# Two layers written out, sums of squares beside the adds, half of the next layer's adaLN weights read beside the router, and half-row scatter-adds

## What is computed

```python
mod = silu(cond) @ w_ada[l] + b_ada[l]              # adaLN: 6 x 1024 numbers per token group
shift1, scale1, gate1, shift2, scale2, gate2 = split(mod, 6)
h = rmsnorm(x, norm1_g) * (1 + scale1) + shift1
proj = h @ w_in[l]                                  # q, k, v, conv, pool, u, v, gates
branches = attention(...), conformer_conv(...), multiscale_pool(...), spatial_gating(...)
x = x + gate1 * (sum(sigmoid(z_gate) * (branch @ w_branch)) @ w_out[l])
h2 = rmsnorm(x, norm2_g) * (1 + scale2) + shift2
aff = softmax(h2 @ w_router[l])                     # 16 experts
gate, idx = top_k(aff.T, 2 * L // 16)               # each expert picks 64 latent and 16 context tokens
y[e] = (silu(h2[idx[e]] @ w1[e]) * (h2[idx[e]] @ w3[e])) @ w2[e] * gate[e]
x = x + gate2 * scatter_add(y, idx)
# after two layers: out = rmsnorm(x, final_g)
```

## Time and profile before

| | us |
|---|---|
| median of 3 runs | 3164.21 |
| lowest, highest | 3155.08, 3170.53 |
| the profiled execution's own time | 3167.31 |
| its span, first to last instruction | 3165.6 |

### The profile page before, as it was taken

How to read it: one execution, slowest core, us unless ns; L and a number is a source line. 1 busy time by engine, 2 the same in 40 slices (tenths; PEclk the granted TensorE clock), 3 DMA queues, 4 the chain that set the end, 5 groups by cost and what they waited for, 6 DMA issues and landing times.

```text
span 3165.6 us, 70846 instructions
## 1 busy us (share of the span) xinstructions
PE 2835.2 (90%) x32596; PEld 2067.1 (65%) x32596; DVE 893.1 (28%) x1513; ACT 495.5 (16%) x862; POOL 270.9 (9%) x290
## 2 busy tenths in 40 slices
PE   6999999999995898998679999999999868898994
PEld 3554576765753788888535456766666458888883
DVE  3953222332114011111159432223221231111113
ACT  3012122332002000000020120233310120000001
POOL 1240000000000001010003200000000000001010
PEclk9999999999997999999889999999999989999997
DMA  7222301012122999999752223011120249999994
GB/s 315 106 113 107 121 30 59 30 56 100 41 80 95 365 401 402 402 401 402 309 222 93 96 107 120 30 59 40 72 87 27 106 168 356 399 405 401 408 403 165
DMA packets 56295, 609.08 MB, mean 192 GB/s; under 512 B 6832, under 2 KB 6832, under 8 KB 22000
## 3 DMA queue, kind: packets, MB, share of 16 engines
q1 hardware_dynamic: 38736, 550.52, 43.2%
q0 software_dynamic: 8448, 24.78, 3.1%
q10 hardware_dynamic: 8992, 32.11, 2.7%
HBM read 577.49 MB, written 29.88 MB: 192 GB/s over the span
## 4 chain that ended last, share of the span: by engine, by line
PE 65%; DMA 23%; DVE 9%; issue 2%; ACT 1%; SPq 0%; POOL 0%; POOLq 0%; DVEq 0%; ACTq 0%
PE ps L292 54%; DMA ring<-in_w_exp 19%; DVE region_b L1047 4%; PE ps L535 2%; DMA ring<-in_w_mix 2%; PE ps L508 1%; PE ps L518 1%; PE ps L589 1%; PE ps L572 1%; PE ps L662 1%; DMA region_x<-ffn_rows 1%; DVE rstd L1004 1%; DMA region_b<-h_rows,rstd 0%; DVE rstd L996 0%; DMA ffn_rows<-region_b,rstd 0%
## 5 line engine op out<-in xcount | busy, mean ns | idle before, releaser
L292 PE MATMUL ps<-hT,ring 128*128 128x320 f32 (+2 forms) x3600 | 1022.3, 442 | 21.5 <-DVE region_b L1035 11.5
L292 PE MATMUL ps<-region_r,ring 128*64 128x80 f32 x24192 | 898.8, 234 | 108.1 <-DMA ring<-in_w_exp 88.7
L292 PEld LDWEIGHTS ps<-region_r,ring 128*64 128x64 f32 x24192 | 867.0, 138 | 141.5 <-DMA ring<-in_w_exp 110.3
L292 PEld LDWEIGHTS ps<-hT,ring 128*128 128x128 f32 x3600 | 612.2, 192 | 382.7 <-issue 239.7
L292 PE MATMUL ps<-region_b,ring 128*128 128x320 f32 (+2 forms) x896 | 257.5, 439 | 3.5 <-DMA ring<-in_w_mix 3.5
L1047 DVE SCALAR_TENSOR_TENSOR region_b<-region_b,params 128x655 f32<-128x655 f32 x240 | 243.9, 1016 | 8.5
L292 PEld LDWEIGHTS ps<-region_b,ring 128*128 128x128 f32 x896 | 159.3, 191 | 75.6 <-issue 23.3
L1354 POOL DMA_INDIRECT region_b<-h_rows,rstd x68 | 62.1, 913 | 1437.4 <-PE ps L671 775.9
L292 PE MATMUL ps<-region_x,ring 128*128 128x512 f32 (+1 forms) x480 | 139.4, 449 | 3.8 <-DVE region_x L1173 3.8
L968 ACT ACTIVATE region_r<-ps 128x320 f32<-128x320 f32 x64 | 28.0, 437 | 640.0 <-PE ps L691 640.0
L1230 DVE COPY region_r<-ps 128x320 f32<-128x320 f32 x64 | 31.5, 492 | 341.2 <-PE ps L691 341.2
(11 more groups left out here) (198 smaller groups left out, 2076.7 us busy)
## 6 DMA issues: line engine op xcount, KB each, us to landing
ring<-in_w_exp SPq DMA_DIRECT2D x180, 2048.0 KB, 10.8
ring<-in_w_mix SPq DMA_DIRECT2D x68, 2048.0 KB, 9.2
ring<-in_w_first SPq DMA_DIRECT2D x8, 2048.0 KB, 8.8
ring<-in_w_last SPq DMA_DIRECT2D x4, 2048.0 KB, 10.2
x_store<-region_m ACTq DMA_DIRECT2D x2, 2560.0 KB, 11.5
ffn_rows<-region_r ACTq DMA_DIRECT2D x4, 1280.0 KB, 17.7
region_m<-x_store ACTq DMA_DIRECT2D x2, 2560.0 KB, 10.4
h_rows<-region_x ACTq DMA_DIRECT2D x10, 512.0 KB, 2.7
```

Source lines behind the costliest of these rows:

```text
L292: ins = pe.matmul(*args, **kw)
```

## The change

All of it is data flow that stays the same in what it computes. In words:

1. The `Fori` over layers is gone: every engine's program has both layers one after the other, semaphores count on over both (`needs`, with the counts of `PER_LAYER`), and there is no barrier and no clearing. The loops over experts stay on PE and SP.
2. At the end of a layer the squares of the new `x` (ACT) and their sum (DVE) stand among the adds of the expert result, as they already did at the output projection; `norm_sum`, root, reciprocal and `normalise` follow at once. It is the same at the end of the second layer for the final norm.
3. The first six adaLN blocks of layer 1 are loaded behind layer 0's output projection (`NEXT_ADA`) and read by PE beside layer 0's router, with their copies on ACT and sums on POOL. Layer 1's own projection has adaLN blocks only in its first six phases. Layer 0 is as before, with four and eight.
4. `turn_h2` uses one PSUM tile, and waits for the copy of the tile before; the other holds the adaLN pieces.
5. SP waits at the layer's end for both loads of `ffn_rows` before it issues layer 1's first weight block.
6. `add_rows` adds 512 columns at a time, 32 times in a layer instead of 16, with a semaphore for each half; `slot_row` is gone.
7. The output is one DVE operation for a tile instead of two.

```diff
+NEXT_ADA = [("ada", _n) for _n in range(ADA_EARLY[1])]
...
-            with sp.Fori(0, LAYERS) as l:
-                for n in range(MIX_BLOCKS):
-                    s = n % SLOTS
-                    load(s, l * per_layer(s) + first_in_slot(n), a["w_mix"][l, n])
...
+            for l in range(LAYERS):
+                if l:
+                    for half in range(2):
+                        sp.wait_ge(S[f"ffn_in{half}"], 16 * l)
+                for n in range(len(MIX_ORDER[l])):
+                    load(MIX_AT[l] + n, a[f"w_mix{l}"][n])
+                if l == 0:
+                    for n, b in enumerate(NEXT_ADA):
+                        load(BLOCK_AT[1][b], a["w_ada"][n])
...
+                need("x_mixed", 2 * KC)
+                next_ada(("rows", 0))
+                norm_sum(("mix", l))
+                next_ada(("turn", 0), ("rows", 1), ("turn", 1), ("rows", 2))
...
-                pe.drain().then_inc(layer_done, 1)
-                pe.wait_ge(layer_go, l + 1)
...
+                norm_sum(("in", l + 1))
...
+                    if e:
+                        sc.wait_ge(rows_added[half], l * (16 * NE) + 16 * e)
...
                 for half in range(2):
+                    sc.wait_ge(rows_added[half], l * (16 * NE) + 16 * NE)
...
+                for k in range(KC):
+                    need("ffn_added", 2 * (k + 1))
+                    square(("in", l + 1), k, x[:, k, :], TOK)
+                root(3 * l + 4, rstd[:, 0:TOK])
...
+                    if k >= 2:
+                        add_square(("in", l + 1), k - 1, TOK)
+                if l + 1 < LAYERS:
+                    v.wait_ge(S["params_in"], 16 * (l + 2))
+                    modulation(l + 1, 0, "g1", mod_next)
+                add_square(("in", l + 1), KC - 1, TOK)
...
-                v.tensor_tensor(h[:, k, :], x[:, k, :], rstd[:, 0:TOK], ALU.mult).then_inc(out_ready, 1)
-                v.wait_ge(out_ready, 2 * k + 1)
-                v.tensor_scalar(h[:, k, :], h[:, k, :], con("final_g", KC)[:, k:k + 1], None, ALU.mult)\
-                    .then_inc(out_ready, 1)
+                v.scalar_tensor_tensor(h[:, k, :], x[:, k, :], con("final_g", KC)[:, k:k + 1], rstd[:, 0:TOK],
+                                       ALU.mult, ALU.mult).then_inc(out_ready, 1)
...
+                def add_rows(j):
+
+                    half = j % 2
+                    need("y_scaled", j + 2)
+                    g.indirect_dma_start(out=a["ffn_rows"], in_=y_tok[:, half * 512:(half + 1) * 512], in_offset=None,
+                                         compute_op=ALU.add,
+                                         out_offset=bass.IndirectOffsetOnAxis(ap=slot_half[:, j:j + 1], axis=0))\
+                        .then_inc(rows_added[half], 16)
```

More of the change, by code:

```diff
@@ L612, in _, with next_ada @@
                     if m % 4 == 3:
-                        read(OUT_BLOCK + m // 4)
-                norm_sum(2 * (KC - 1) + BC - 1)
+                        read(block_at["out", m // 4])
+                def next_ada(*steps):
+                    for step, n in steps:
+                        if l + 1 == LAYERS:
+                            return
+                        if step == "rows":
+                            ada_rows(l + 1, n, PS[1])
+                        else:
+                            pe.wait_ge(S["ada_part_in"], ADA_BLOCKS * (l + 1) + n)
+                            ada_turn(l + 1, n, PS[1], ada_row_next)
+                need("x_mixed", 2 * KC)
+                next_ada(("rows", 0))
+                norm_sum(("mix", l))
+                next_ada(("turn", 0), ("rows", 1), ("turn", 1), ("rows", 2))
                 for k in range(KC):
-                    pe.wait_ge(S["h_ready"], 2 * (KC + k + 1))
+                    pe.wait_ge(S["h_ready"], 2 * (KC * NORM_AT["mix", l] + k + 1))
                     at = PAR["router"] + k * NE
@@ L637, in _ @@
                 turn_h2(0)
[L638 to L640 removed]
+                need("logit_rows", 1)
                 for t in range(TT):
@@ L649, in _ @@
                 last.then_inc(S["aff_turned"], 1)
-                for t in range(2, TT):
-                    turn_h2(t)
-                pe.wait_ge(S["best_found"], 1)
+                turn_h2(1)
+                next_ada(("rows", 3))
+                turn_h2(2)
+                turn_h2(3)
+                next_ada(("turn", 3))
+                turn_h2(4)
+                next_ada(("rows", 4), ("turn", 4), ("rows", 5), ("turn", 5))
+                need("best_found", 1)
                 pe.transpose(PS[3][0:CAP, 0, 0:NE], best, ident[0:NE, 0:NE])
@@ L738, in _ @@
                 assert not pending
-                pe.drain().then_inc(layer_done, 1)
-                pe.wait_ge(layer_go, l + 1)
-            pe.wait_ge(final_add, KC - 1)
-            over_partitions(PS[0], rstd, columns("half"), final_sum)
+                norm_sum(("in", l + 1))
+            pe.wait_ge(cond_ready, 1)
+            for l in range(LAYERS):
+                layer(l)
         @block.scalar
@@ L1027, in conv_input, with layer @@
+            def layer(l):
+                need = needs(v, l)
+                if l == 0:
+                    for k in range(1, KC):
+                        add_square(("in", 0), k, TOK)
+                    normalise(("in", 0), 1)
+                    need("params_in", 16)
+                    modulation(0, 0, "g1", mod3)
+                need("pads_zero", 1)
                 def conv_input(c):
-                    v.wait_ge(S["conv_sig"], 2 * (c + 1))
+                    need("conv_sig", 2 * (c + 1))
@@ L1322, in _ @@
                                          ALU.subtract), "pool_d")
-                for n in range(ADA_FIRST + 3, ADA_BLOCKS):
-                    ada_sum(n)
-                g.wait_ge(S["conv_norm"], 2 + BC)
+                for n in sums[sums.index(first) + 1:]:
+                    ada_sum(l, n, mod3)
+                need("conv_norm", 2 + BC)
                 g.memset(prob[:, :, 0:64], 0.0).then_inc(S["prob_pad"], 1)
```

825 lines of the change are left out of this document (435 added, 390 removed).

## The result

| | before | after |
|---|---|---|
| median, us | 3164.43 (4 runs) | 3120.26 (4 runs) |
| lowest, highest | 3155.08, 3170.53 | 3116.62, 3120.74 |
| the profiled execution's own time | 3167.31 | 3116.62 |

The ratio is 0.9862, with a 95% interval of 0.9842 to 0.9882: 44 us or 1.4% less, where 39.8 were forecast (3124.4). Two later series of the same kernel gave medians of 3115.93 and 3118.54.

A forecast was written before the change was run, and what follows sets the result against it. DMA bounds the experts, PE the projections and gates, serial waits the layer ends and router. Terms -29.9 - 9.9 - 5.0 - 1.0 + 1.0 + 5.0 = -39.8 give a median of 3124.4 us, range 3110 to 3142.

The forecast's parts named there:

- Step (c): Layer 0's end: the load of half 0 of the sums lands in 6.05 us, so PE starts at 1557.2.
- step (e): Layer 0's end: DVE's adds and sums of squares take 14.4 us, to 1573.0; the last sum ends at 1574.0.
- It fits: Layer 0's end: half 1 of the sums is loaded by 1562.6, before tile 4 needs it at about 1565.
- The modulation: Layer 0's end: DVE's 0.4 us for the new modulation hides in the wait for ACT's last square.
- (d): Layer 0's end: first transposes to DVE's first add take 1.4 us, so DVE starts at 1558.6.
- (f): Layer 0's end: from `norm_sum` to the reciprocal's end takes 8.4 us, to 1582.4.
- (g): Layer 0's end: one `normalise` tile, two ACT pieces and gaps take 2.1 us; PE starts layer 1 at 1584.5.
- the six steps: Layer 0's router: adaLN rows, copy, turn, copy and POOL sum; last turn at about 1002 to 1008.2, against 1006.95.
- My rival of a late router: Layer 0's router: PE slow, handshakes add up, gather collides with a weight block; 8 us more, 3132; chance 0.11.
- The reason that I gave for a half: Experts: 5 us lost, half of the middle case, since ordinary fetches of the same 2 KB share q0's extra time.
- The rivals of dear adds: Experts: half-row adds cost +32 us (3151, chance 0.10), or 75 at the lone price (3194, slower, chance 0.04).
- The rival of more gain: Whole kernel: the experts' loop costs nothing and PE enters layer 1 at full clock, 3116; chance 0.06.

The follow-up runs named there:

- whole_rows: Changed kernel with scatter-adds by whole rows again, 16 of 1024 columns in a layer: 3131.10 us.
- no_hold: Changed kernel, but SP does not wait for the loads of the sums before issuing layer 1's first weight blocks: 3125.31 us.
- squares_after: Changed kernel, but at both layers' ends ACT squares x only after all adds and DVE sums the squares after that: 3125.61 us.
- rows_two_late: Changed kernel with the third adaLN block's products behind layer 0's router products instead of ahead of them: 3125.10 us.

## Why the prediction was right, point by point

**Layer 0's end (-29.9; measured -27.8 in the first pair, -28.1 by the means).** The right mechanism, sized 2 us too high. Step (c): half 0's load, issued at 1543.10, reached PE 7.0 us later, not 6.05. In step (e) "It fits" is wrong: the last add took 6.17 us and not 5.0, beside the load of half 0, and half 1's load 7.33 and not 6.1, so half 1 came 13.6 after the last add's issue instead of 11.2, and DVE stood for 0.87. I had taken both durations from the program's end of before, where they run alone. The modulation did not hide either: ACT's last square was ready before DVE was free, so DVE's 0.4 for it lie on the path. Steps (d), (f) and (g) measured 1.34, 8.4 and 2.3 against 1.4, 8.4 and 2.1, and DVE's pitch 2.03 against 2.02. Which part of the change is worth how much is shown in part only. In this stage `whole_rows`, `no_hold` and `squares_after` lose 4.4, 5.6 and 2.8 us. No run brings the barrier or the adaLN blocks at the layer's start back, so that they cost what the chain of before has them for is read from the chain, not shown.

**The program's end (-9.9; -10.3).** From the last add's issue to `norm_sum` 22.8 us, where the steps gave 3137.5 - 3114.80 = 22.7. The output took 6.46 against 7.1: an operation with three operands lasts 0.88, as I had it, but the next one starts 0.80 after it.

**Layer 1's projections (-5.0).** 5.0 to 5.4 without q's first tile. In the traces of after the stage gained 3.6 on the mean, because the first tile of q ran at the lower clock in all three (10.3 to 10.5 us instead of 8.6), as it did in nine of the twelve traces of after and its variants, while before's two have 8.6 and 8.9.

**Router (-1.0 in layer 1; +1.0 in layer 0).** Layer 1 has -0.6. Layer 0 has +0.1, but the steps behind it were not all as I had them. PE waited 3.02 us for the third adaLN block and started the router's products at 965.41 instead of about 963.5; the six steps were over at 995.3, 2.7 us ahead of their limit, on PE's side. DVE's last operation even ends 1.05 us earlier in the stage than before, and that is lost again: 0.8 by the later fetch, 0.4 by a gather of 3.4 instead of 3.0. What I had not seen is the stores of `h_rows`: the last goes from 2.7 us to 9.4 beside the weight blocks, and the first fetch is issued 0.8 us later than DVE alone would have had it. My rival of a late router had 0.11 and "collides with a weight block" in its list. It did not come, but the three variants that move a single step of PE show a loss of 6 to 7 us.

**Experts (+5; +2.3 by stretches with a spread of 3 to 4, at most 5.3 by q0's shares).** q0's share went from 7.9% to 8.4%, under the 9% named. A row more took 0.033 engine-us, which is just the half of 0.067 that I took. The reason that I gave for a half, that the fetches are in the extra too, names no size, so the closeness of this term is luck. The rivals of dear adds, at 32 and 75 us, fall. By the rule of the Trainium skill (DMA: Bandwidth & Descriptors, section Anatomy of one DMA) 2.0 us for each of 32 more adds would have been 64 us, and here at most 5.3 of them count in the full loop. That fits the same section's remark that this time is mostly the wait for the receipt, but no run here shows what it is spent on.

The sum by the means of spans is -42.5, against -39.8. Of these, 2.2 lie in layer 0 ahead of its router, where nothing was forecast and where two executions of the same kernel differ by up to 9 us. The other stages add up to -40.2. That this is within half a microsecond of the forecast is luck in part: the two ends and layer 1's projections and router gained 3.2 us less than forecast, and the experts and layer 0's router lost 3.6 less. The rival of more gain named 3116, and the three series lie at 3116 to 3120, but not by its mechanism: PE did not come into layer 1 at full clock (0.80 over the first 9.8 us of after's projections).

## What to carry to other kernels

A serial end of a stage is worth a term-by-term forward sum from its last handover: the pieces here came within 1 us each wherever their durations were taken from a place with the same DMA neighbours, and up to 2.4 us off where not. A transfer's duration belongs to the traffic beside it: before work is moved beside a quiet stretch, list the small transfers there that someone waits for, and keep the big blocks away from them. Before a difference between two profiles is explained, take a second profile of each.

## What was unexpected of the hardware

A 512 KB store landed in 2.7 us alone, in 9.4 beside one or two weight blocks of 2 MB, and in 13.0 in rows_two_late; a gather of 80 half rows in 2.9 to 3.4 or in 9.3 to 9.5. So a small transfer can pay about the time that a block in flight needs (5.2 at 402 GB/s) and more.

The Trainium skill (DMA: Bandwidth & Descriptors, section Queues, rings and completion order) has each engine take turns between queues packet by packet. Counted in the profile's packets, the trace agrees. From 992.5 to 998.0 in after the last store (q10) ran beside weights (q1):

```profile
q1 hardware_dynamic: 127, 1.84, 78.0%
q10 hardware_dynamic: 127, 0.52, 22.9%
```

Both moved 127 packets, but one of the weights has 14.5 KB on average and one of the store 4.1. So 512 KB of store are about as many packets as a block of 2 MB, and the store doesn't finish ahead of it. From these rows a packet of the store takes 0.229 x 5.5 x 16 / 127 = 0.16 engine-us and one of the weights 0.54. An estimate: 128 packets of the store are 8 on each of the 16 engines, 8 x 0.70 = 5.6 us with as many packets of weights between them, and 1.3 without. That is 4.3 of the 6.7 us by which the store landed later.

An add of whole rows that runs alone costs the engines more than its two halves. The queue in 5.0 us around layer 0's last add of whole_rows:

```profile
q0 software_dynamic: 96, 0.33, 46.2%
```

in 8.0 us around the program's last half add of after:

```profile
q0 software_dynamic: 96, 0.16, 11.4%
```

That is 0.462 x 5.0 x 16 = 37 engine-us for 80 rows of 4 KB, as in the earlier trace rows, and 0.114 x 8.0 x 16 = 14.6 for 80 of 2 KB: two halves are 29. But the half add runs beside the load of half 0. In the 10.0 us from 1551.3 in before, a whole-row add ran beside weights and loads:

```profile
q0 software_dynamic: 96, 0.33, 16.4%
```

That is 26 engine-us for the same 80 rows of 4 KB, less than two halves. So it may be the lone add that is dear, and not the whole row; no run has a half add alone, and why is open.
